# Two transformer layers on one core: output products taken by token tile, with the lows of the weights handed over in pieces

## The reference

```python
# first layer
h = h + rmsnorm(mixed @ w_out, norm_mix_post)         # mixed: 512 x 1024
hn = rmsnorm(h, norm_x_pre); mn = rmsnorm(mem, norm_mem)   # mem: 256 x 1024
qx = hn @ w_q_x;  kx, vx = jnp.split(mn @ w_kv_x, 2, axis=-1)
# cross attention over mem gives ox
h = h + rmsnorm(ox @ w_o_x, norm_x_post)
hn = rmsnorm(h, norm_ffn_pre)
g, up = jnp.split(hn @ w_gate_up, 2, axis=-1)         # 2816 wide each
h = h + rmsnorm((jax.nn.silu(g) * up) @ w_down, norm_ffn_post)
# second layer, h is its x
z = rmsnorm_2(x, g_mix) @ w_in                        # mLSTM, window attention, memory, three gates
y = (gates[:, :, 0] * (h_m @ w_proj_mlstm) + gates[:, :, 1] * (h_na @ w_proj_na)
     + gates[:, :, 2] * (h_mem @ w_proj_mem))
x = x + y @ w_out
return x + jnp.square(jax.nn.relu(rmsnorm_2(x, g_ffn) @ w_up)) @ w_down
```

## Time and profile before

| | |
|---|---|
| Median of three runs | 1980.76 us (1980.16 to 1982.06) |
| Profiled execution | 1979.19 us |
| Its span, first to last instruction | 1977.5 us |
| Mean granted clock of TensorE | 0.927 |
| TensorE busy | 1789.3 us, 90% |
| VectorE, ScalarE, GpSimd busy | 36%, 34%, 37% |

### The profile page before, as it was taken

The page is one execution under the profiler, slowest core; times in us unless marked ns, Lnnn a source line. Parts: engine busy times, 40 slices in busy tenths (PEclk is TensorE's granted clock), DMA queues, the critical chain, the costliest instruction groups (busy, mean ns, idle before and its releaser), DMA issues. The chain is left out here.

```text
span 1977.5 us, 22030 instructions
## 1 busy us (share of the span) xinstructions
PE 1789.3 (90%) x8211; PEld 1433.3 (72%) x8211; DVE 703.3 (36%) x1421; ACT 678.1 (34%) x989; POOL 722.4 (37%) x638
## 2 busy tenths in 40 slices
PE   7999969897996999999968899998978979999999
PEld 6987748676765878878847676666766768888887
DVE  6414775324315111101146164453455432222131
ACT  4113455344325233222233334332434333232231
POOL 5123203344231444554424434333313435444453
PEclk9869979898997999999978999997889989999999
DMA  4142201122121233233213223232123422232321
GB/s 156 64 128 74 66 1 65 64 86 76 64 86 43 86 106 85 86 125 99 65 43 96 85 86 103 77 89 73 49 74 112 146 64 86 86 107 85 107 86 64
DMA packets 163027, 165.14 MB, mean 84 GB/s; under 512 B 25713, under 2 KB 125160, under 8 KB 162920
## 3 DMA queue, kind: packets, MB, share of 16 engines
q1 hardware_dynamic: 140440, 147.18, 23.5%
q10 hardware_dynamic: 22480, 16.56, 2.9%
HBM read 155.33 MB, written 8.40 MB: 83 GB/s over the span
## 5 line engine op out<-in xcount | busy, mean ns | idle before, releaser
L681 POOL TENSOR_TENSOR w_low<-raw,w_high 128x512 fp32r<-128x512 f32 x513 | 673.2, 1343 | 1123.0 <-ACT w_high L792 1122.6
L1927 PE MATMUL bank<-xT_high,w_high 128*128 128x512 f32 x1016 | 419.1, 412 | 15.3 <-DVE xT_low L1299 13.1
L1928 PE MATMUL bank<-xT_low,w_high 128*128 128x512 f32 x1016 | 405.4, 399 | 0.0
L1929 PE MATMUL bank<-xT_high,w_low 128*128 128x512 f32 x1016 | 405.0, 399 | 0.0
L792 ACT CAST w_high<-raw 128x2048 fp32r<-128x2048 f32 x131 | 245.1, 1871 | 287.5 <-PE bank L1929 266.6
L1927 PEld LDWEIGHTS bank<-xT_high,w_high 128*128 128x128 f32 x1016 | 196.6, 194 | 71.9 <-issue 14.8
L1929 PEld LDWEIGHTS bank<-xT_high,w_low 128*128 128x128 f32 x1016 | 196.6, 193 | 43.3
L1928 PEld LDWEIGHTS bank<-xT_low,w_high 128*128 128x128 f32 x1016 | 197.4, 194 | 38.4
L1927 PE MATMUL bank<-w_high,hid_high 128*128 128x512 f32 x432 | 172.1, 398 | 3.7 <-POOL w_low L681 3.7
L1928 PE MATMUL bank<-w_low,hid_high 128*128 128x512 f32 x432 | 172.1, 398 | 0.0
L1929 PE MATMUL bank<-w_high,hid_low 128*128 128x512 f32 x432 | 171.9, 398 | 0.0
(11 more groups left out here) (363 smaller groups left out, 2402.1 us busy)
## 6 DMA issues: line engine op xcount, KB each, us to landing
raw<-in_w_in SPq DMA_DIRECT2D x33, 1024.0 KB, 5.2
raw<-in_w_down SPq DMA_DIRECT2D x26, 1024.0 KB, 5.0
raw<-in_w_gate_up SPq DMA_DIRECT2D x44, 512.0 KB, 5.1
raw<-in_w_up SPq DMA_DIRECT2D x16, 1024.0 KB, 5.2
raw<-in_w_kv_x SPq DMA_DIRECT2D x8, 1024.0 KB, 5.4
raw<-in_w_out SPq DMA_DIRECT2D x8, 1024.0 KB, 5.1
sg<-gate_dram ACTq DMA_DIRECT2D x8, 768.0 KB, 4.5
gate_dram<-qbuf ACTq DMA_DIRECT2D x20, 256.0 KB, 2.0
```

The costliest lines, as they stand in the source:

```text
L681: ins = pool.tensor_tensor(low[:, cs], full[:, cs], high[:, cs], ALU.subtract)
L1927: pe.matmul(ps, ah, bh, start=first, stop=False)
L1928: pe.matmul(ps, ah, bl, start=False, stop=False)
L1929: return pe.matmul(ps, al, bh, start=False, stop=last)
```

## The change

**Order of chunks and tiles.** `out` and `vx` are interleaved in the plan: out 0, left half of vx (two chunks), out 1, out 2, out 3, right half of vx. For `out`, `ox`, `down2` and `out2` a function `by_token` runs chunk 3 one token tile behind chunk 2, with the turn of a tile as soon as it may be there. `first_tiles` then runs the first tiles of the next product (four of gu0 and up0, three of if and qk2) over the first 256 tokens only, with the turns of tokens 2 and 3 between them, and after that over the other 256.

**The tail.** `post_halves` replaces `post`: ScalarE squares each half straight from its bank, VectorE multiplies it by the post gain into `ynat`, and one fused instruction scales and adds to h. The gain of hx, hf, h2 and h4 is loaded as a row over all partitions (`gnat`) and multiplied in when `stage` is written, so ScalarE casts the high part and VectorE subtracts straight from the transposed bank, without `qbuf`.

**Lows in pieces.** `wl_done` counts pieces of 512 columns. TensorE makes a tile's products with `w_high` first, then those with `w_low`, waiting for each piece.

**Homes.** The first chunk of gu0, of if and of up0 has buffers of its own outside the ring.

**Gates.** `sg` has a third buffer, gates are asked for two ahead, and the casts for the next `proj2` chunk stand earlier. Some small gain loads on SyncE's queue move.

The core of the diff:

```diff
+HOMES = {"gu0": 0, "if": 0, "up0": 1}
+NATURAL = ("hx", "hf", "h2", "h4")
-    p.rows("out", a["w_out"], 0, 2, 4)
-    p.rows("vx", a["w_kv_x"], 1024, 2, 2, readers="X")
+    p.row_chunk(out, a["w_out"], 0, lower, halves[0])
+    p.row_chunk(vx, a["w_kv_x"], 1024, lower, left)
+    p.row_chunk(vx, a["w_kv_x"], 1024, upper, left)
+    p.row_chunk(out, a["w_out"], 0, upper, halves[0])
+    p.row_chunk(out, a["w_out"], 512, lower, halves[1])
+    p.row_chunk(out, a["w_out"], 512, upper, halves[1])
+    p.row_chunk(vx, a["w_kv_x"], 1536, lower, right)
+    p.row_chunk(vx, a["w_kv_x"], 1536, upper, right)
...
                         ins = pool.tensor_tensor(low[:, cs], full[:, cs], high[:, cs], ALU.subtract)
+                        if o + LOW < width:
+                            own.mark(ins, wl_done)
                     own.tell(ins, wl_done)
...
+            def post_halves(group, yname, hname, src_ready, following, filler=None):
...
+                for j in range(ST):
+                    i = STATS.index((yname, j))
+                    if j == ST - 1:
+                        high(following.n + 1)
+                    square(4 + j, rms[:, i:i + 1])
+                    own.tell(act.activation(rms[:, i:i + 1], rms[:, i:i + 1], ACT.Sqrt, bias=rms[:, 56 + j:57 + j],
+                                            scale=1.0 / D), rms_done)
+                    if filler and j == ST - 1:
+                        high(filler.n)
+                    if j:
+                        hi(ntile[hname, j - 1])
+                    residual_stat(hname, j, src_ready)
...
+                for j in range(ST):
+                    k = STATS.index((yname, j))
+                    take(4 + j)
+                    scale(4 + j)
+                    dve.wait_ge(rms_done, k + 1)
+                    own.link(dve.reciprocal(rms[:, k:k + 1], rms[:, k:k + 1]))
+                    own.tell(dve.scalar_tensor_tensor(out=h[:, j, :], in0=ynat[:, j, :], scalar=rms[:, k:k + 1],
+                                                      in1=h[:, j, :], op0=ALU.mult, op1=ALU.add), h_ready)
+                    if j:
+                        lows(hname, j - 1)
+                    xn(hname, j, D)
+                lows(hname, 3)
...
+            def by_token(name, xh, xl, phase, first=0, low=None, base=0):
...
+                product(c[2], 0, xh, xl)
+                for j in range(1, ST):
+                    product(c[2], j, xh, xl)
+                    product(c[3], j - 1, xh, xl)
+                    if j >= 2:
+                        turn(phase, j - 2)
+                product(c[3], ST - 1, xh, xl)
...
+            def first_tiles(tiles, phase):
+
+                turned_ready(phase, 2)
+                for i, (c, k) in enumerate(tiles):
+                    product(c, k, xTh, xTl, part=(0, S // 2))
+                    if i < 2:
+                        turn(phase, 2 + i)
+                low_all(phase)
+                for c, k in tiles:
+                    product(c, k, xTh, xTl, part=(S // 2, S))
...
                         elif g.mode == "N":
+                            js = slice(m * P, (m + 1) * P)
                             for q, k in enumerate(ks):
-                                js = slice(m * P, (m + 1) * P)
-                                mm = three(ps[:, :], xh[:, k, js], xl[:, k, js], ch[:, q, :], cl[:, q, :],
-                                           first and q == 0, last and q == len(ks) - 1)
+                                pe.matmul(ps[:, :], xh[:, k, js], ch[:, q, :], start=first and q == 0, stop=False)
+                                pe.matmul(ps[:, :], xl[:, k, js], ch[:, q, :], start=False, stop=False)
+                            for q, k in enumerate(ks):
+                                low_ready(c, q)
+                                mm = pe.matmul(ps[:, :], xh[:, k, js], cl[:, q, :], start=False,
+                                               stop=last and q == len(ks) - 1)
```

More of the change, by code:

```diff
@@ L239, in norm_tiles @@
         for j in range(ntok):
-            out.append((phase, j, banks, base, kt0, gain))
+            out.append((phase, j, banks, base, kt0, gain, scaled))
             base += banks
+            if phase not in NATURAL:
+                scaled += banks
     return out
@@ L1875, in _ @@
                     dve.wait_ge(gate_ready, 2 * cp + m + 1)
+                    gate = [g[:, k, :] for g, b0, b1 in sg(2 * cp + m) for k in range(b1 - b0)]
                     for b in range(3):
```

417 lines of the change are left out of this document (269 added, 148 removed).

## The result

The changed kernel takes 1897.5 us (median of four, 1891.4 to 1904.7) where the kernel before takes 1981.0: a ratio of 0.958, 95% interval 0.954 to 0.962. Two later comparisons gave 0.953 (0.950 to 0.955, median 1892.8) and 0.955 (0.952 to 0.958, median 1892.6). All ratios and medians leave out runs more than 1.5% above the fastest of the same kernel, which stand in the ranges only. The forecast was 1893.5. The profiled execution took 1891.38 us for a span of 1889.7, 87.8 less than before; the sum of the forecast was 87.3.

The account below looks back on a forecast made before the run. Time was taken as matmuls at 0.23 us plus TensorE's idle time plus low-clock matmuls. Gains 21.9+16.7+12.7+12.5+15.1+8.4 = 87.3 us from 1979.19 give 1892, plus 1.6 for the median 1893.5; forecast 1875 to 1912 (0.56), range 1864 to 1934.

Parts of the forecast that it names:

- A: Output product, values of the memory, turn to hx: 33.9 us lost, 14.0 would remain, gain 21.9.
- E: Gated products: 12.7 us lost, 5.3 would remain, gain 8.4 from the third gate buffer and earlier casts.
- F: Elsewhere: 14.6 us of waits for w_low plus 4.5 of low clock, 4 would remain, gain 15.1 from pieces.
- B: Tail after ox: 20.7 us lost plus 2.0 of low clock, 6.0 would remain, gain 16.7.
- the term for GpSimd's interference: After ox: VectorE's fused operations slowed while GpSimd subtracts, 1.2 us per token, put in as 1.8.
- rival 1: VectorE paces the tails at about 9 us per token; gain only 45, time 1936; chance 0.24.
- C: Tail after down2: 26.1 us lost plus 2.0 of low clock, 15.4 would remain, gain 12.7.
- D: Tail after out2, without a second norm: 12.0 us lost plus 2.0 of low clock, 1.5 would remain, gain 12.5.
- TensorE 3.23 for the banks behind (1529.76, named issue): Gated products: TensorE waits 3.23 us for banks behind late gates; asking two gates ahead gives 11 us for their return.
- rival 3: The low clock holds through the staggered stretches, 672 matmul lengths costing 134 us more, time 2028; chance 0.03.
- Rival 2: The tails close entirely, short waits covered and low clock gone from all but one place; gain 110, 1871; chance 0.12.
- Rival 4: The waits move: the weight stream comes late and TensorE's gain is lost, time 1979; chance 0.02.

Follow-up runs that it names:

- the kernel before with pieces: The kernel before with only the lows handed over in pieces and products with w_high of a tile first: 1951.5 us, ratio 0.988.
- the repetition: The changed kernel measured again with no edit: 1892.8 us, ratio 0.953.
- Early casts: The changed kernel with several ScalarE casts and the root's table load moved earlier in its order: 1882.7 us, ratio 0.946.
- gates as before: The changed kernel with two gate buffers, gates asked for one ahead, and the proj2 casts where they were: 1898.3 us, ratio 0.957.
- whole lows: The changed kernel, but TensorE waits for all pieces of a chunk's lows before the chunk's first matmul: 1952.9 us, ratio 0.982.
- tails dense: The changed kernel, but in ox, down2 and out2 chunk 2 runs for all token tiles, then chunk 3: 1916.9 us, ratio 0.964.
- one gate ahead: The changed kernel with three gate buffers but gates asked for one ahead in place of two: 1902.4 us, ratio 0.960.
- second repetition: The changed kernel measured once more with no edit: 1892.6 us, ratio 0.955.

## Why the prediction was right

The forecast of 87.3 us met 87.8, and the steps can be checked one by one. Stages A to E came within 1 us each, but that the total is met to 0.5 us is luck: F gave 5.3 more than forecast, and the head took 3.5.

*What bounds.* That the time is matmuls at 0.23 us plus idle time plus low clock held: 66.1 us of idle time went (184.7 to 118.6 over the span, by adding TensorE's gaps) and 21.6 of busy time.

*A, 21.9 forecast, 21.4 measured.* The waits of 3.5 and 2.9 for casts are 3.58 and 3.03, turn 0's 1.2 is 0.81. Pieces alone give 11.0 of it; of the rest the interleaving is 6.9 by one profile, mostly at its end, ahead of qx, and not ahead of chunk 1 of out; the last 3.5 no run isolates.

*B, 16.7 and 16.2.* Turn 0 waited 2.08 (forecast 1.8), the first half tile 0.93 (0.7), turn 3 2.43 (1.7). The last carries the term for GpSimd's interference. VectorE's two fused operations for token 3 in the changed kernel:
```profile
591.34 2.02 DVE L1690 SCALAR_TENSOR_TENSOR h<-ynat,rms,h 128x1024 f32<-128x1024 f32 x1
...
595.23 1.59 DVE L1390 SCALAR_TENSOR_TENSOR stage<-h,rms,gain_natural 128x1024 f32<-128x1024 f32 x1
```
and GpSimd beside them, three of its four pieces of lows, one by one:
```profile
591.00 1.28 POOL L752 TENSOR_TENSOR w_low<-raw,w_high 128x512 fp32r<-128x512 f32 x1
...
592.23 2.28 POOL L752 TENSOR_TENSOR w_low<-raw,w_high 128x512 fp32r<-128x512 f32 x1
...
594.47 1.26 POOL L752 TENSOR_TENSOR w_low<-raw,w_high 128x512 fp32r<-128x512 f32 x1
```
Both wait. The operation that started at 591.34, when 0.94 us of a piece were left, took 0.74 more than its 1.28; the one at 595.23, with 0.50 of a piece left, took 0.31 more; and the piece that started at 592.23, under the first operation, took 1.00 more than its 1.28. That makes 1.05 us on the path for two operations, where I had put 1.8. Over the tails of A, B and C (shortest, median and longest in ns):
```profile
L1390 DVE SCALAR_TENSOR_TENSOR stage<-h,rms,gain_natural x12: 1283/1285/2103, 421.2 to 991.4; 128x1024 f32<-128x1024 f32 x12
```
```profile
L1690 DVE SCALAR_TENSOR_TENSOR h<-ynat,rms,h x12: 1284/1285/2018, 418.0 to 987.5; 128x1024 f32<-128x1024 f32 x12
```
Seven of the 24 started while a piece was running, and each of the seven took longer, by what was left of the piece less 0.20 us (0.29 to 0.82, 4.0 us in all); the other 17 met no piece and took 1.28 to 1.29. The Trainium skill, SBUF — State Buffer, section Who interferes with whom, calls the port pair that the two engines share an exclusive lock, and this trace agrees. The 21 us that the prediction worked out from it did not come for another reason: it charged every operation of A and B a whole piece, and in those two tails five of sixteen met one, for 3.0 us together, the 3 that the sum had counted. So rival 1 fell because GpSimd is idle beside most of the tails; of six waits for `stage` one was over 4 us.

*C, 12.7 and 12.0.* With the pieces' share taken from the kernel before with pieces (223.1 to 210.0), C's own is 210.0 to 198.0 (196.4 in the repetition). Its inside was not as forecast. Turn 0 waited 5.03 (forecast 4.0), the first half tile 3.15 (2.9), but turns 1 and 3, for which I had put 4.5, next to nothing (0.42), and two pieces of qk2's lows 1.75 that were not in the sum. Turn 0's extra is a wait that I had not seen. ScalarE and GpSimd in the changed kernel:
```profile
963.03 0.30 ACT L870 CAST home_high<-raw 128x128 fp32r<-128x128 f32 x1 [5.77 <-POOL home_low L743]
963.36 0.63 ACT L1051 ACTIVATE junk<-ynat 128x512 bf16<-128x512 f32 x1
...
961.88 1.04 POOL L743 CAST home_low<-small 128x1024 fp32r<-128x1024 f32 x1
```
The square of token 0 stands behind the cast into the home of `if`, and this behind GpSimd's zeroing of it, 1.3 us after its input was there (961.37 and 0.69 for VectorE's sum). Early casts took this away.

*D, 12.5 and 13.1.* Right in size: no wait above 0.8.

*E, 8.4 and 7.5: right number, wrong wait.* The step that failed is "TensorE 3.23 for the banks behind (1529.76, named issue)". I took it for a wait for banks that VectorE frees late since gates come late. It was one for the whole of `w_low`, like the one of 2.25 behind it. ScalarE and GpSimd in the kernel before:
```profile
1519.20 1.49 ACT L1230 ACTIVATE sg<-sg 128x1536 f32<-128x1536 f32 x1 [5.31 <-DMA sg<-gate_dram]
...
1521.79 1.91 ACT L792 CAST w_high<-raw 128x2048 fp32r<-128x2048 f32 x1
...
1523.84 5.81 POOL L681 TENSOR_TENSOR w_low<-raw,w_high 128x512 fp32r<-128x512 f32 x4 [12.34 <-ACT w_high L792]
```
The last piece ends at 1529.65, TensorE starts at 1529.76. The late gate did have a part in it, by another way than I thought: the cast stands in ScalarE's queue behind a sigmoid that had waited 5.31 for its gates. So there are two cures, and each is enough alone: pieces without the gate part (E 46.3 in the kernel before with pieces, 46.1 with gates as before), and the gate part with whole lows (46.2). With neither it is 53.6. The gain of 7.5 can't be divided between them, and which of the gate part's three edits (third buffer, two ahead, earlier casts) makes it a cure is open. The earlier casts have besides a use that I had not counted, 4 us at the start of out2.

*F, 15.1 and 20.4.* 7.3 in F1 and, by the kernel before with pieces, 13.1 in F2. Two terms were mis-sized. The 4 us left over were 2.2: four waits for pieces of 0.34 to 0.73. And the low clock behind F's waits, put at 4.5 for two of them, was 7.0 behind four: after the waits of 1.87 (727.66), 3.15 (861.54), 1.84 (997.46) and 4.28 (1091.74) in the kernel before, matmuls start 0.42 apart and cost 1.5 to 2.3 us each time; only the one of 2.90 (1118.94) cost nothing, as the prediction had it. The waits of 1.87 and 1.84 are short and stand alone, so the low clock is not found only where waits stand close or are long, as rival 3 had it.

*The head, 0 and -3.5.* Not in the forecast. In the repetition of the same kernel the head was 4.3 shorter, so chance alone can make such a difference.

*Rivals.* Rival 1 is answered under B. Rival 2, tails that close entirely, did not come: waits of up to 5.03 us remain in A, B and C. Rival 3, a low clock that holds through the staggered stretches, did not come: the granted clock is 0.93, 0.93, 0.84 and 1.00 in A, B, C and D. Rival 4 did not either: the full stretches run as before, and no wait for `w_high` stands outside A.

## What to carry over

When a product waits for a helper's output that is made in pieces, hand over the pieces and do first what does not need them; this pays once in the waits that stand in the profile and once more by letting work start inside other stages' tails, and only taking it away again from the finished kernel shows the second half. Two parts of a change can each be enough to end the same wait: take out either and nothing returns, so before one of them gets the credit, look at a kernel with neither. A tail of a norm is best covered by work that needs half of it (the first 256 tokens), more than by an earlier end of its first token. And a wait called "issue" has no cause in the trace: before a cause is assigned, look which semaphores the instruction waits for, and which of them belong to an engine that finished just then; and if that engine was late, what stood before it in its queue.

## What the runs showed that was not expected

*A low clock without any idle time.* In the stretch of window attention the same instructions take two courses. Windows of the changed kernel, and of the one with early casts at the same place of the program:
```profile
1335.30:1355.30 20.00, 19.02 (x109) 15.57 (x108) 9.42 (x26) 10.12 (x20) 0.60 (x1) 0.71 0.04 14
1355.30:1375.30 20.00, 19.48 (x122) 16.50 (x124) 7.18 (x21) 8.00 (x19) 4.37 (x4) 0.86 0.21 66
```
```profile
1317.60:1337.60 20.00, 20.00 (x85) 16.78 (x83) 4.80 (x14) 5.60 (x12) 0.00 (x0) 0.50 0.00 1
1337.60:1357.60 20.00, 20.00 (x101) 16.19 (x101) 8.74 (x25) 8.95 (x17) 1.75 (x2) 0.62 0.04 14
```
At 1.2 GHz TensorE is itself the bound there and never waits; at 2.4 GHz it waits for the others now and then. The stretch from the first qkT product to hmT takes 294.6 to 302.5 us in eleven of the profiles and 311.5, 312.8 and 313.9 in three (tails dense, one gate ahead, early casts), none of which changed it. The products of 24 columns in the head behave alike: 18.8 us in one profile of the changed kernel and less in another (the first mark behind them at 96.8 and 94.5), at 0.50 with TensorE fully busy. Why the clock goes one way or the other is open; no experiment was made on it. A single profile can be 13 us off by it, and it is a likely part of the spread of the times: in the second repetition the mean granted clock was 0.952 in the fastest run (1889.9) and 0.932 in the slowest (1919.0).

*The same wait, and the low clock at once or later.* The wait of 3.58 for the first chunk of vx was followed by a matmul of 0.77 in one execution of the changed kernel, and by one of 0.47 in the next. Timeline of that second one, the first matmul and the seventh:
```profile
378.06 0.47 PE L2155 MATMUL bank<-w_high,memT_high 128*128 128x512 f32 x1 [3.58 <-ACT w_high L870]
...
379.62 0.63 PE L2155 MATMUL bank<-w_high,memT_high 128*128 128x512 f32 x1
```
The low clock came all the same, 1.5 us later: from the seventh on matmuls start 0.43 apart. Over the whole first chunk it cost 2.9 us in the one and 2.3 in the other. The wait of 3.03 likewise gave 0.79 in the first and 0.50 in the second, and there the low clock began 1.6 us later. A wait of 3.15 (983.32) cost nothing, the halved matmuls behind it start 0.12 apart, and one of 2.08 was followed by seven matmuls 0.43 apart (from 576.19), though the transposes right behind it ran at full clock. So in these traces the length of a wait between 2 and 4 us does not tell whether and when the low clock follows. In all it cost some 39 us over the changed kernel's span and some 55 in the kernel before, added up from matmuls of 512 columns that start over 0.36 us apart.
